# The last modulation columns on VectorE during QKV, and a tenth place for expert matrices

## The chip, the cores and the metric

The kernel runs on one core of one Trainium2 chip. The metric is the device time of one execution in microseconds, lower is better. All arithmetic is float32.

## The reference, cut to what matters

Two layers over 256 context and 256 latent tokens of width 1024 (512 rows, four tiles of 128). Layer 0 mixes tokens with a bidirectional Mamba-2 SSD, layer 1 with differential attention; each is followed by a mixture of 16 experts, two per token. Every sub-layer is modulated by six vectors per layer, made from the conditioning:

```
mod_l = silu(c)     @ ada_w[i] + ada_b[i]      # latent tokens, 6 * 1024 columns
mod_c = silu(c_ctx) @ ada_w[i] + ada_b[i]      # context tokens
sh1, sc1, g1, sh2, sc2, g2 = split(mod_l, 6)
hl  = rmsnorm(xl) * (1 + sc1) + sh1            # before the mixer
xl  = xl + g1 * mixer(hl)
hl2 = rmsnorm(xl) * (1 + sc2) + sh2            # before the experts
xl  = xl + g2 * experts(hl2)
```

In the second layer only latent rows leave the mixer, so of its columns g1, sh2, sc2 and g2 only the row of `c` is used. An expert has three matrices of 2 MB: gate, up (1024 x 512) and down (512 x 1024).

## The kernel before, in words

The program is written by hand, one instruction stream for each engine (TensorE `pe`, VectorE `v`, ScalarE `act`, GpSimd `pool`, and `sp`, the queue that issues nearly all loads). Each stream runs in its written order; semaphores join them. Nothing plans or reorders. The stages follow each other: modulation and first norm (to some 125 us), the SSD walk (to 456), output projection (to 580), first experts (to 830), QKV (844 to 990), attention (to 1085), second experts (to the end).

**The modulation columns.** The 12,288 columns are six groups q of 2048 (q = 0 to 2 are layer 0, q = 3 to 5 layer 1). Group 0 is made at the start. Groups 1 to 5 are made in the SSD walk in 40 pieces: piece p has 128 rows of `ada_w` and 2048 columns (1 MB, two loads of 512 KB by `ada_piece_sync`, L326, into two alternating buffers), and four products on TensorE add it into bank 7 of PSUM (`ada_piece_tensor`, L334; 32 output rows, of which two are used, latent and context; each float32 product shows as two records). After eight pieces VectorE adds the bias (`ada_vector`, L344) and ScalarE stores the rows to `mod_d` in memory (`ada_scalar`, L353). Later stages load from `mod_d`.

**The walk.** 16 iterations i, one for each 128 channels. On TensorE one has a projection of x (L822), the transposes (L843), the states (L866), a projection of z (L833), and the outputs (L882, L886). `ada_turn` (L675) puts a piece at three turns of an iteration: after the projection of x, after that of z, and after the outputs; every ninth turn is skipped. The same turns stand in `fused_sync` on `sp`, where the third comes after the load of the decay rows of iteration i + 2, which waits for the outputs of iteration i.

**Experts.** Class `Moe` sorts the rows into groups of 128 slots (ten in the first stage, seven in the second), and each group uses one to four experts. The 48 matrices of a stage are loaded once each, in an order of first use (`seq`), into nine places of 2 MB: six of `ring`, and parts of other buffers (`SLOTS`, `SLOTS + 1`, `NINTH` in the first stage, `SPLIT`, in three pieces, in the second). `sync_first` (L1742) loads those of experts 0 to 2, whose number doesn't depend on the routing, each behind the wait that frees its place; `sync_rest` (L1750) loads the others when the routing is known (`PERM`, `WEIGHTS`), each after the last use of the matrix that was in its place. In the first stage eight matrices are loaded ahead and `NINTH` takes the ninth after the routing; in the second the ninth goes to `SPLIT` after the routing.

**QKV** (`att_tensor`, L2577). 20 products of 128 x 512 outputs (L2591), m_ = 0 to 19: query halves for the two latent tiles, key halves and value halves for four tiles. After products 12 to 17 come the transposes of one normed query or key tile each (L2562), after 18 and 19 the first scores. VectorE (`att_vector`, L2708) norms and rotates six tiles, n = 0 to 5: two of queries (ready after products 2 and 3), four of keys (products 8 to 11; n = 2, 3 are context and aren't rotated). GpSimd gives the reciprocal roots between. `att_sync` (L2515) loads the six weight blocks, then the two of the output projection, then a gate row.

## Time and profile before

| | us |
|---|---|
| median of 3 runs | 1308.67 (1308.54 to 1314.22) |
| the profiled execution's own time | 1307.49 |
| its span | 1305.8 |
| TensorE busy | 1241.2 (95%) |
| VectorE busy | 555.7 (43%) |
| ScalarE busy | 376.3 (29%) |
| GpSimd busy | 200.7 (15%) |
| moved by DMA | 347.86 MB, mean 266 GB/s |
| mean granted clock of TensorE | 0.993 of full |

How to read it: the span is the time from the first to the last instruction; the profiled execution took 1.7 us more than its span. "Idle before, releaser" is the time an engine stood still in front of an instruction, and what ended it. In a row of windows the numbers after the stretch are its length and the busy time of TensorE's products, of its weight loads, of VectorE, ScalarE and GpSimd, each with its count; then the granted clock, the busy share of the 16 DMA engines, and GB/s.

### The profile page before, as it was taken

Reading aid. Unit: us, or ns where it says so; the run is one execution under the profiler, and the core shown is the slowest. Engines: PE = TensorE matmul, PEld = TensorE weight load, DVE = VectorE, ACT = ScalarE, POOL = GpSimd, SP = SyncE. Lnnn points to the kernel's source line nnn. Section 1 sums busy time; section 2 is a strip of 40 time slices with the busy share of each in tenths; the row PEclk is TensorE's granted clock in tenths of the full one; section 3 lists DMA queues with packets and bytes.
Section 4 is the critical chain, followed back from the end, with each engine's and each line's share of the span. In section 5 each row is a group of like instructions: output and inputs, shape, how many; then the busy total and the mean of one; then the engine's idle time right before and its main releaser. Section 6 shows DMA issues by size and latency. Waiting matters only on the chain.

```text
span 1305.8 us, 14975 instructions
## 1 busy us (share of the span) xinstructions
PE 1241.2 (95%) x5951; PEld 580.8 (44%) x5951; DVE 555.7 (43%) x907; ACT 376.3 (29%) x706; POOL 200.7 (15%) x192
## 2 busy tenths in 40 slices
PE   5899999999999999999999998899999899999977
PEld 3344444444454444574343432344444556444322
DVE  1448375756657412462111111662606755232213
ACT  2334666575756400111010100320115521000000
POOL 1001234343434310001000000311200300000000
PEclk9999999999999999999999999999999999999989
DMA  9334557766575583089999999970006237999997
GB/s 359 113 133 153 182 203 260 257 236 238 190 259 177 210 323 129 32 352 372 426 427 426 427 430 426 390 281 1 1 16 266 110 126 315 423 426 426 425 416 292
DMA packets 81454, 347.86 MB, mean 266 GB/s; under 512 B 9721, under 2 KB 27817, under 8 KB 66657
## 3 DMA queue, kind: packets, MB, share of 16 engines
q1 hardware_dynamic: 74603, 327.47, 64.1%
q10 hardware_dynamic: 4268, 10.44, 2.1%
q0 software_dynamic: 2512, 8.97, 1.7%
q8 instruction: 48, 0.79, 0.3%
q14 instruction: 23, 0.19, 0.0%
HBM read 337.67 MB, written 9.18 MB: 266 GB/s over the span
## 4 chain that ended last, share of the span: by engine, by line
PE 78%; DMA 9%; DVE 7%; SPq 2%; ACT 2%; issue 1%; ACTq 1%; POOL 0%; DVEq 0%; POOLq 0%
PE psum L1801 21%; PE psum L2591 11%; PE psum L822 10%; PE psum L833 8%; PE psum L1169 6%; DMA ring<-in_moe_w_down 5%; PE psum L340 3%; PE psum L1885 2%; PE psum L2643 2%; PE psum L866 2%; PE psum L886 2%; SPq L1773 1%; DMA arena<-mod_d 1%; PE psum L1939 1%; PE psum L882 1%
## 5 line engine op out<-in xcount | busy, mean ns | idle before, releaser
L1801 PE MATMUL psum<-ring,arena 128*32 128x512 f32 (+2 forms) x1504 | 318.6, 603 | 10.0 <-DMA ring<-in_moe_w_down 7.5
L1801 PEld LDWEIGHTS psum<-ring,arena 128*32 128x32 f32 (+2 forms) x1504 | 96.0, 125 | 175.1 <-issue 158.5
L822 PE MATMUL psum<-hT,ring 128*128 128x512 f32 x384 | 169.7, 596 | 0.0
L2591 PE MATMUL psum<-ring,hT 128*128 128x512 f32 x320 | 138.9, 592 | 0.0
L1169 PE MATMUL psum<-ring 128*128 128x512 f32 x256 | 112.1, 594 | 4.2 <-DVE X L1229 2.9
L833 PE MATMUL psum<-hT,ring 128*128 128x512 f32 x256 | 112.5, 592 | 0.0
L822 PEld LDWEIGHTS psum<-hT,ring 128*128 128x128 f32 x384 | 71.3, 190 | 91.3 <-issue 91.3
L1801 PE MATMUL psum<-arena 128*32 128x512 f32 (+2 forms) x304 | 109.3, 594 | 0.0
L1027 DVE SCALAR_TENSOR_TENSOR arena<-arena,cols 128x512 f32<-128x512 f32 x96 | 92.8, 966 | 3.4
L2591 PEld LDWEIGHTS psum<-ring,hT 128*128 128x128 f32 x320 | 60.1, 190 | 73.0 <-issue 72.2
L2011 ACT ACTIVATE arena<-psum 128x512 f32<-128x512 f32 x17 | 18.2, 1068 | 215.4 <-PE psum L1801 215.4
L965 ACT ACTIVATE ring<-ring,dts 128x128 f32<-128x128 f32 x256 | 76.5, 387 | 0.5
L1169 PEld LDWEIGHTS psum<-ring 128*128 128x128 f32 x256 | 47.8, 190 | 62.5 <-issue 56.6
L833 PEld LDWEIGHTS psum<-hT,ring 128*128 128x128 f32 x256 | 47.4, 190 | 53.6 <-issue 53.6
L2060 DVE TENSOR_TENSOR arena<-arena,psum 128x512 f32<-128x512 f32 x17 | 18.2, 1069 | 108.5 <-PE psum L1801 108.5
L1801 PE MATMUL psum<-hT,arena 128*64 128x512 f32 (+2 forms) x144 | 63.5, 594 | 0.0
L1057 DVE COPY X<-psum 128x256 f32<-128x256 f32 x16 | 6.8, 424 | 107.0 <-PE psum L866 107.0
L1801 PEld LDWEIGHTS psum<-arena 128*32 128x32 f32 (+2 forms) x304 | 31.3, 126 | 42.6 <-issue 42.3
L2671 ACT ACTIVATE arena<-psum 128x512 f32<-128x512 f32 x20 | 11.9, 597 | 116.6 <-PE psum L2591 116.6
L1115 POOL TENSOR_TENSOR arena<-arena,dts 128x512 f32<-128x512 f32 x32 | 39.1, 1243 | 38.3 <-ACT arena L947 38.3
L1106 POOL TENSOR_TENSOR ring<-ring,arena 128x512 f32<-128x512 f32 x16 | 20.3, 1271 | 148.1 <-ACT ring L958 148.1
L340 PE MATMUL psum<-arena,X 128*32 128x512 f32 x240 | 42.4, 605 | 0.0
(360 smaller groups left out, 1588.7 us busy)
## 6 DMA issues: line engine op xcount, KB each, us to landing
ring<-in_moe_w_gate SPq DMA_DIRECT2D x23, 2048.0 KB, 16.6
ring<-in_moe_w_up SPq DMA_DIRECT2D x22, 2048.0 KB, 18.0
ring<-in_moe_w_down SPq DMA_DIRECT2D x20, 2048.0 KB, 21.6
arena<-in_ada_w SPq DMA_DIRECT2D x60, 512.0 KB, 5.9
ring<-in_ssd_w_in SPq DMA_DIRECT2D x16, 1024.0 KB, 8.1
ring<-acs_d SPq DMA_DIRECT2D x16, 1024.0 KB, 7.0
ring<-in_da_w_in SPq DMA_DIRECT2D x6, 2048.0 KB, 16.5
ring<-in_ada_w SPq DMA_DIRECT2D x20, 512.0 KB, 5.1
```

The lines of the kernel that those rows point to most:

```text
L340: m = pe.matmul(psum[32 * j:32 * j + 32, 7, :], c_sil[:, k, :], ada_buf[p % 2][j // 2][:, (j % 2) * NB:(j % 2 + 1) * NB], start=(k == 0), ...
L822: mm = pe.matmul(psum[:, bank, :], w_[:, k, c0:c0 + P], hT[:, k, :], start=(k == 0), stop=(k == KD - 1))
L833: mm = pe.matmul(psum[:, 1, :], zw[b % 2][:, k, (i % 2) * P:(i % 2 + 1) * P], hT[:, k, :], start=(k == 0), stop=(k == KD - 1))
L866: mm = pe.matmul(dst, Bt[:, c_, g * STATE:(g + 1) * STATE], src, start=True, stop=True)
L886: mm = pe.matmul(dst[r, :], S[:, lv, P * d_ + 64 * hh:P * d_ + 64 * hh + 64], EC[i % 2][:, n, hh * P:(hh + 1) * P], start=False, stop=(las ...
L965: m = act.activation(x_, x_, ACT.Relu, scale=-1.0, bias=ebias[:, b:b + 1])
L1027: ins = v.scalar_tensor_tensor(out=o, in0=u_[:, :, tap:tap + SEG], scalar=cols[:, t_:t_ + 1], in1=o, op0=ALU.mult, op1=ALU.add)
L1115: pool.tensor_tensor(out=XW[:, :, n, :].rearrange("p c (h e) -> p c h e", h=2), in0=xtok[:, i % 2].rearrange("p c (h e) -> p c h e", h=2), ...
L1169: mm = pe.matmul(psum[:, wout_bank(n), :], yT[:, k, t * P:(t + 1) * P], slot((4 + k // KD, k // KD)[half], KD)[:, k % KD, :], start=(k == ...
L1801: mm = pe.matmul(psum[rows, dst, :], lhsT[:, k, rows], weight(s_, a, k, part), start=(k == 0), stop=(k == a - 1))
L1885: m = pe.matmul(psum[:, k // 4, (k % 4) * P:(k % 4 + 1) * P], self.norm.rows[t][:, k * P:(k + 1) * P], (token_mask[j] if n else self.mask0 ...
L2591: mm = pe.matmul(psum[:, 4 + m_ % 2, :], hT[:, k, t * P:(t + 1) * P], slot(qkv_slot[n], KD)[:, k, :], start=(k == 0), stop=(k == KD - 1))
```

## The change

Five things change.

- The pieces of groups 4 and 5 (16 of 40) leave the walk. The other 24 are placed at the first turn of each iteration and the second turn of every even one. The three copies come at i = 5, 10, 15.
- Groups 4 and 5 are made in QKV, for the latent row alone. `sp` loads 1 MB pieces into the two halves of a new buffer `spare`; VectorE multiplies each by the column of `silu(c)` (one number for each partition) and adds it into `late_acc` (128 x 2048, in the part of X that held context tiles). After eight pieces TensorE sums over the partitions by four products with ones, VectorE adds the bias and `sp` stores the row. TensorE waits for pieces 0 to 7 after product 9, for 8 to 15 after product 18.
- `spare` is also the tenth place for expert matrices, and the first to be filled in both stages.
- Room for it: the triangle matrices and the columns move into X, `ones` becomes a broadcast column, the strict triangle of the router comes from memory instead of a subtraction, and the descriptor space of GpSimd's DMAs becomes 2048 bytes.
- Small things that follow: a third SiLU at the start (`c_keep`), a wait of `sp` for the last transposed product before X is reloaded, a wait of GpSimd for the stored rows.

```diff
-        tri_up = sb("tri_up", [P, P])
-        tri_lo = sb("tri_lo", [P, P])
-        ones = sb("ones", [P, P])
-        cols = sb("cols", [P, 176])
+        spare = sb("spare", [P, SLOT])
+        c_keep = small[:, 24:32]
+        tri_up, tri_lo = X[:, 1, 768:768 + P], X[:, 1, 768 + P:D]
+        cols = X[:, 2, 0:176]
+        ones = small[:, 16:17].broadcast_to([P, P])
...
+            act.activation(c_keep, cols[:, CC0:CC0 + KD], ACT.Silu).then_inc(csil_ready, 1)
...
-        PIECES = 5 * KD
+        PIECES, WALKED = 3 * KD, 3
+        ADA_COPY = {5: 1, 10: 2, 15: 3}
...
         def ada_turn(do, eng, p, i, n):
-            if (3 * i + n) % (KD + 1) == KD or p >= PIECES:
+            if n == 2 or (n == 1 and i % 2) or p >= PIECES:
                 return p
...
-            sp.wait_ge(mod_out, 160)
+            sp.wait_ge(mod_out, 32 * WALKED)
...
+            sp.wait_ge(yT_ready, NT)
             sp.dma_start(X[:, 2:4, :], x[0].rearrange("(t p) n -> p t n", p=P)).then_inc(x_back, 16)
...
+                eng.dma_start(self.strict, strict_d).then_inc(self.s["router_in"], 16)
...
-                   ((0, 1), (0, 2), (1, 1), (1, 2), (0, 0), (1, 0), (2, 1), (2, 2)),
-                   (4, 5, 0, 2, 1, 3, 7, 6, NINTH), (2, 2, 1, 1, 2, 2, 0, 0, 0, 0), None, None, (nA, nS, ngb, nh, njunk))
+                   ((0, 1), (0, 2), (1, 1), (1, 2), (0, 0), (1, 0), (2, 1), (2, 2), (2, 0)),
+                   (SPARE, 4, 5, 0, 2, 1, 3, 7, 6, NINTH), (2, 2, 1, 1, 2, 2, 0, 0, 0, 0, 0), None, None, (nA, nS, ngb, nh, njunk))
...
+        def late_piece_sync(sp, p):
+            q, k = WALKED + 1 + p // KD, p % KD
+            if p >= 2:
+                sp.wait_ge(ada_used, PIECES + p - 1)
+            sp.dma_start(late_buf(p), ada_w[1, k * P:(k + 1) * P, (q % 3) * 2 * D:(q % 3 + 1) * 2 * D]).then_inc(ada_in[p % 2], 16)
...
+        def late_piece_vector(v, p):
+            q, k = WALKED + 1 + p // KD, p % KD
+            v.wait_ge(ada_in[p % 2], 32 * (PIECES // 2) + 16 * (p // 2) + 16)
+            if k == 0:
...
+                v.tensor_scalar(late_acc, late_buf(p), c_keep[:, k:k + 1], None, ALU.mult).then_inc(ada_used, 1)
+            else:
+                v.scalar_tensor_tensor(out=late_acc, in0=late_buf(p), scalar=c_keep[:, k:k + 1], in1=late_acc, op0=ALU.mult,
+                                       op1=ALU.add).then_inc(ada_used, 1)
+            v.wait_ge(ada_used, PIECES + p + 1)
+
+        def late_sum_tensor(pe, q, bank):
+            n = q - WALKED
+            pe.wait_ge(ada_used, PIECES + KD * n)
+            for j in range(4):
+                m = pe.matmul(psum[32 * j:32 * j + 32, bank, :], small[:, 16:17].broadcast_to([P, 32]), late_acc[:, j * NB:(j + 1) * NB],
+                              start=True, stop=True)
+            m.then_inc(ada_done, 1)
...
+            sp.wait_ge(*moe0.used(*moe0.holder[SPARE]))
+            for p in range(2):
+                late_piece_sync(sp, p)
             for n in range(2):
                 sp.wait_ge(A["qkv_mm"], (2, 4)[n])
                 load(sp, out_slot[n], blocks(da_w_out[0], n * NB), KD)
+            for p in range(2, LATE):
+                late_piece_sync(sp, p)
+                if p == 2:
+                    ada_bias_sync(sp, WALKED + 1)
+                if p == LATE - 1:
+                    late_store_sync(sp, WALKED + 1)
+                    ada_bias_sync(sp, WALKED + 2)
+            moe1.sync_first(sp, 0, ([(ada_used, PIECES + LATE)],))
+            late_store_sync(sp, WALKED + 2)
+            sp.wait_ge(mod_out, 32 * WALKED + 32)
...
+        LATE_SUM = {9: (WALKED + 1, 2), 18: (WALKED + 2, 7)}
+        LATE_VECTOR = ((0,), range(1, KD), (), range(KD, KD + 2), range(KD + 2, KD + 4), range(KD + 4, LATE))
...
+                if m_ in LATE_SUM:
+                    late_sum_tensor(pe, *LATE_SUM[m_])
                 if m_ >= FIRST_V:
+                    if m_ == FIRST_V:
+                        pe.wait_ge(ada_copied, WALKED + 2)
...
+        def late_vector(v, n):
+            if n == 2:
+                late_copy_vector(v, WALKED + 1, 2)
+            for p in LATE_VECTOR[n]:
+                late_piece_vector(v, p)
...
-                   qkv_slot[2:6] + [7] + out_slot + [6, SPLIT], [f + 1 + (s_ in out_slot) for s_, f in enumerate(qkv_fill[0:SLOTS])] + qkv_fill[SLOTS:SLOTS + 2] + [0], moe0, norm_b,
+                   [SPARE] + qkv_slot[2:6] + [7] + out_slot + [6, SPLIT],
+                   [0 if s_ == SPLIT else f + (s_ in qkv_slot) + (s_ in out_slot) for s_, f in enumerate(qkv_fill)], moe0, norm_b,
...
-            moe0.sync_first(sp, 0, ([(wo_mm, TT)], [], [(wo_mm, 2 * TT)], [], [(wo_mm, 2 * TT + 1)], []))
+            moe0.sync_first(sp, 0, ([], [(wo_mm, TT)], [], [(wo_mm, 2 * TT)], [], [(wo_mm, 2 * TT + 1)], []))
...
-            moe1.sync_first(sp, SLOTS + 2, ([moe1.routed("PERM")],))
...
-    nc = bacc.Bacc("TRN2", target_bir_lowering=False, num_devices=1)
+    nc = bacc.Bacc("TRN2", target_bir_lowering=False, num_devices=1, dynamic_dma_scratch_size=2048)
```

## Rows read from the trace of the kernel before

**Rows 1.** the page: busy times by engine, and GB/s in 40 slices of 32.6 us

```profile
PE 1241.2 (95%) x5951; PEld 580.8 (44%) x5951; DVE 555.7 (43%) x907; ACT 376.3 (29%) x706; POOL 200.7 (15%) x192
...
GB/s 359 113 133 153 182 203 260 257 236 238 190 259 177 210 323 129 32 352 372 426 427 426 427 430 426 390 281 1 1 16 266 110 126 315 423 426 426 425 416 292
```

**Rows 2.** waits of TensorE: 125:490 (first), 580:850 (two), 1080:1306 (last)

```profile
PE psum L340 <- DMA arena<-in_ada_w: 2.0, 1, 2.0
...
PE psum L1985 <- DVE hT L2295: 2.5, 1, 2.5
PE psum L1801 <- DMA ring<-in_moe_w_down: 1.7, 1, 1.7
...
PE psum L1801 <- DMA ring<-in_moe_w_down: 5.8, 2, 3.9
```

**Rows 3.** chain of waits, 278:322: start us, us, what

```profile
278.37 7.06 PE psum L822 x16
...
295.20 1.00 PE psum L340 x8
...
299.52 7.07 PE psum L822 x16
...
319.68 2.34 PE psum L822 x5
```

**Rows 4.** timeline, 299:322: VectorE, ScalarE

```profile
309.52 0.42 DVE L1057 COPY X<-psum 128x256 f32<-128x256 f32 x1 [7.79 <-PE psum L866]
...
301.83 0.63 ACT L939 ACTIVATE arena<-arena 128x512 f32<-128x512 f32 x1 [5.84 <-DVE arena L1074]
```

**Rows 5.** chain of waits, near the walk's end

```profile
421.54 4.87 DMA arena<-in_ada_w
```

**Rows 6.** chain of waits, at the start

```profile
13.71 0.31 ACT X L275 x2
```

**Rows 7.** chain of waits over the whole span, QKV stage

```profile
859.82 75.54 PE psum L2591 x176
```

**Rows 8.** timeline of VectorE, QKV stage

```profile
890.73 1.22 DVE L2740 TENSOR_TENSOR arena<-arena 128x1024 f32<-128x1024 f32 x1
```

**Rows 9.** by source line: ns min/median/max of each form

```profile
L1027 DVE SCALAR_TENSOR_TENSOR arena<-arena,cols x96: 750/752/1808, 56.5 to 420.5; 128x512 f32<-128x512 f32 x96
...
L2295 DVE SCALAR_TENSOR_TENSOR hT<-hT,arena x2: 1283/1283/1283, 827.7 to 831.4; 128x1024 f32<-128x1024 f32 x2
...
L2294 DVE TENSOR_SCALAR hT<-hT,arena x2: 753/754/754, 826.9 to 830.6; 128x1024 f32<-128x1024 f32 x2
```

**Rows 10.** transfers: of line L332, and the DMA issues in 843:1000

```profile
DMA to landing us min/median/max: 3.6/5.7/11.8
...
ring<-in_da_w_out SPq DMA_DIRECT2D x2, 2048.0 KB, 8.0
```

**Rows 11.** timeline of TensorE, 1245:1252

```profile
1250.70 1.93 PE L1801 MATMUL psum<-ring,arena 128*32 128x512 f32 x8 [3.85 <-DMA ring<-in_moe_w_down]
```

**Rows 12.** windows: stretch, us, busy by engine, PEclk, DMA share, GB/s

```profile
1250.00:1256.00 6.00, 5.30 (x36) 1.41 (x40) 0.00 (x0) 0.00 (x0) 0.00 (x0) 0.64 0.99 421
795.00:800.00 5.00, 3.29 (x8) 0.77 (x8) 0.00 (x0) 0.00 (x0) 0.00 (x0) 0.69 1.03 436
```

**Rows 13.** windows of the expert stages, same columns

```profile
495.00:555.00 60.00, 60.00 (x173) 28.97 (x172) 20.74 (x47) 7.40 (x13) 2.23 (x6) 1.00 0.22 88
...
600.00:790.00 190.00, 190.00 (x1012) 70.47 (x1012) 29.54 (x42) 17.84 (x25) 6.54 (x7) 1.00 1.01 427
...
1100.00:1290.00 190.00, 179.71 (x1192) 70.91 (x1192) 49.80 (x98) 9.31 (x11) 0.00 (x0) 0.98 1.01 421
```

**Rows 14.** chain of waits, at the end

```profile
1277.93 14.20 DMA ring<-in_moe_w_down
```

**Rows 15.** gathers: timeline of GpSimd, 795:845, and the chain

```profile
817.17 0.95 POOL L2263 DMA_INDIRECT hT<-moe_y_d,arena  x1 [88.22 <-DMA moe_y_d<-arena]
...
818.42 7.90 DMA hT<-moe_y_d,arena
```

More of the change, by code:

```diff
@@ L136, in slot @@
         def slot(s, a):
-            flat = ring[:, s, :] if s < SLOTS else {SLOTS: arena[:, 4096:8192], SLOTS + 1: hT[:, :, :].rearrange("p k t -> p (k t)"), NINTH: arena[:, 0:4096]}[s]
+            flat = ring[:, s, :] if s < SLOTS else {SLOTS: arena[:, 4096:8192], SLOTS + 1: hT[:, :, :].rearrange("p k t -> p (k t)"), NINTH: arena[:, 0:4096], SPARE: spare[:, :]}[s]
             return flat.rearrange("p (a b) -> p a b", a=a)
@@ L144, in backbone @@
         up_d = nc.inline_tensor(np.triu(np.ones((P, P), np.float32)), "up_d").ap()
+        strict_d = nc.inline_tensor(np.triu(np.ones((P, P), np.float32), 1), "strict_d").ap()
         lo_d = nc.inline_tensor(np.tril(np.ones((P, P), np.float32)), "lo_d").ap()
@@ L148, in backbone @@
         full = [sem(f"slot{s}_full") for s in range(SLOTS + 3)]
-        SPLIT, NINTH = SLOTS + 2, SLOTS + 3
-        full.append(full[SPLIT])
+        SPLIT, NINTH, SPARE = SLOTS + 2, SLOTS + 3, SLOTS + 4
+        full += [full[SPLIT], sem("spare_full")]
         def split_pieces():
@@ L252, in setup_pool @@
         def setup_pool(pool):
-            pool.memset(ones[:, :], 1.0).then_inc(pool_set, 1)
             pool.memset(small[:, :], 0.0).then_inc(pool_set, 1)
             pool.memset(Xflat[:, 0:256], 0.0).then_inc(pool_set, 1)
-            pool.wait_ge(pool_set, 3)
+            pool.wait_ge(pool_set, 2)
+            pool.memset(small[:, 16:17], 1.0).then_inc(pool_set, 1)
             pool.memset(mhalf, -0.5).then_inc(pool_set, 1)
@@ L300, in keep_busy @@
             for _ in range(n):
-                pe.matmul(psum[:, bank, 0:P], ident[:, :], ones[:, :], start=True, stop=True)
+                pe.matmul(psum[:, bank, 0:P], ident[:, :], ident[:, :], start=True, stop=True)
         def ada_first_tensor(pe):
@@ L345, in ada_vector @@
             v.wait_ge(ada_used, KD * q)
-            v.wait_ge(adab_in, 16 + 64 * (3 if q <= 3 else 5))
+            v.wait_ge(adab_in, 16 + 64 * WALKED)
             if q == 1:
@@ L697, in fused_sync @@
                 ada_piece_sync(sp, p)
-            for q in range(1, 4):
+            for q in range(1, WALKED + 1):
                 ada_bias_sync(sp, q)
@@ L1007, in fused_scalar @@
                     conv_copy(act, BCN + i + 2)
-                if i and i % 3 == 0:
-                    ada_scalar(act, i // 3)
                 if i + 1 < NT:
@@ L1013, in fused_scalar @@
                     z_scalar(act, i + 1)
+                if i in ADA_COPY:
+                    ada_scalar(act, ADA_COPY[i])
             yT_scalar(act, NT - 1)
@@ L1091, in fused_vector @@
                     gated_vector(v, step, i - 1)
-                if i and i % 3 == 0:
-                    ada_vector(v, i // 3)
+                if i in ADA_COPY:
+                    ada_vector(v, ADA_COPY[i])
                 states_vector(v, step, i)
@@ L1183, in wout_tensor @@
             for t_ in range(TT):
-                mm = pe.matmul(psum[:, 3, t_:t_ + 1], acc[:, t_ * P:(t_ + 1) * P], ones[:, 0:1], start=True, stop=True)
+                mm = pe.matmul(psum[:, 3, t_:t_ + 1], acc[:, t_ * P:(t_ + 1) * P], small[:, 16:17], start=True, stop=True)
             mm.then_inc(y_scale, 1)
@@ L1481, in shift_tensor @@
                 pe.wait_ge(cols_ready, self.cols_at + 1)
-                pe.matmul(psum[:, self.bank, 256:256 + NE * len(self.conds)], ones[:, :], self.rwR.rearrange("p c e -> p (c e)"), start=True, stop=True)
+                pe.matmul(psum[:, self.bank, 256:256 + NE * len(self.conds)], ones, self.rwR.rearrange("p c e -> p (c e)"), start=True, stop=True)
             def router_pool_start(self, pool, step):
@@ L1751, in sync_rest @@
                 expert = {r: r for r in range(NPRE)}
-                for m, r in self.seq[len(self.slots) - (not self.masked):]:
+                for m, r in self.seq[len(self.slots) - 1:]:
                     if len(expert) == NPRE:
@@ L1761, in sync_rest @@
                         sp.wait_ge(*self.used(*self.after[(m, r)]))
-                    else:
+                    elif not self.masked:
                         sp.wait_ge(*self.routed("WEIGHTS"))
@@ L2529, in att_pool @@
             pool.wait_ge(A["small_in"], 144)
-            pool.memset(mhalf16, -0.5).then_inc(A["const"], 1)
-            pool.wait_ge(A["const"], 1)
+            step(pool.memset(mhalf16, -0.5))
             for n in range(6):
@@ L2726, in att_vector @@
                     ins.then_inc(done, 1)
+                    late_vector(v, n)
                     continue
```

55 lines of the change are left out of this document (36 added, 19 removed).

## The prediction

> **What bounds the kernel now.** I read the page's busy shares first: TensorE is busy for 95% of the span [rows 1]. So time can go only where TensorE does less or waits less. The chain of waits, then asked for by stretch, shows one line after another of TensorE with hardly an idle piece. The waits of TensorE give the rest: 2.0 us in the SSD walk, a few in the first mixture of experts, and in the second several for transfers, of which the largest group is 5.8 us [rows 2] and all four together are 11.6 us. So the walk is bound by what TensorE issues, each expert stage is bound by TensorE at first and by its weights at the end, and the QKV stage by TensorE alone.
>
> **The change part by part.** The frame is the profiled execution: span 1305.8 us, its own time 1307.5 us; the median of the runs is 1.2 us above that.
>
> **1. The walk.** One piece (four column products, eight records) takes 1.00 us of the chain [rows 3]. An iteration with three pieces lasts 299.52 - 278.37 = 21.15 us, one with two 319.68 - 299.52 = 20.16 us [rows 3]: the difference is the piece itself, nothing hides it. 40 pieces become 24, so 16 x 1.00 = 16.0 us go. New iterations hold two pieces or one (20.16 and 19.16 us). Does something else become late there? VectorE waits 7.8 us for the states of this iteration and ScalarE 5.8 us for the gated product [rows 4]; both wait for TensorE's course, so a loss of 1.0 to 2.0 us an iteration stays inside that slack. The second to last piece waits 2.0 us for its transfer, because a DMA of the third turn is issued only after the outputs of its iteration; the chain shows it as a DMA piece of 4.87 us [rows 5]. The new walk has no third turn: every piece is asked for at least a third of an iteration before its use. That is another -2.0. The three copies move to iterations 5, 10 and 15; two of them now wait for a piece of their own iteration, but what follows on VectorE is the state copy, which waits for a later product anyway: 0. SP's queue loses 32 half-pieces and two bias loads: 0, it waits for TensorE.
>
> **2. Start.** A third SiLU of 8 columns stands before the squares on ScalarE. Two take 0.31 us and the squares follow at once on the chain [rows 6]: +0.2. The missing memset, broadcast ones, and the triangle matrix from memory: 0 (bounds -0.5 and +0.5).
>
> **3. The late pieces in QKV.** TensorE gets two sums, each four products of the form of a piece: +2.0. The pieces are work of VectorE now, and TensorE waits for them at one point: after product 9 of 20 it needs pieces 0 to 7. In the trace of before, products 2 to 12 run back to back from 859.82 in 75.54 us, 6.87 us each [rows 7]; product 9 ends at 859.82 + 8 x 6.87 = 914.8. VectorE ends its second query tile at 890.73 + 1.22 = 891.95 [rows 8]. A piece with its addition is a form that costs 0.75 us for 512 columns and 1.28 us for 1024 [rows 9], so 0.53 for each further 512, and 2.34 us for 2048. Piece 0 needs no addition; that form does 1024 columns in 0.75 us [rows 9], so 1.3 us for 2048. It stands before the second query tile, so the run of pieces 1 to 7 starts at 891.95 + 1.3 = 893.3. Piece 1 is there and is used at 895.7. Piece 3 could be asked for only now, since there are two buffers, and each later pair again waits for its own buffer: transfer plus use per pair. A transfer of 1 MB: a half of 512 KB lands in 3.6 us at least and 5.7 in the median, a 2 MB one on an idle queue in 8.0 [rows 10]; 512 KB cost 1.2 us at the rate of 427 GB/s [rows 13], so 3.6 + 1.2 = 4.8 from one side and 8.0 - 2.5 = 5.5 from the other. I take 5.2. Three pairs then take 3 x (5.2 + 2.34 + 0.1 issue) = 22.9, and piece 7 is used at 918.6: TensorE waits 918.6 - 914.8 = +3.9 us, a pace of 3.8 us a piece. Bounds: 0, with 3.6 us a transfer; 12, with 8.0 and with the 3 us that 2048 columns would cost if contention made them a quarter slower. I stay near the rows of this size.
>
> By the Trainium skill ("DMA: Bandwidth & Descriptors", Anatomy of one DMA) a transfer costs some 2.0 us plus its bytes over 436 GB/s, so 4.4 us here as an estimate; the stall would be 1.5 us. Its Bandwidth section has 6.15 us for 1 MB, which would make 6.7 us. No row here shows a lone transfer of 1 MB in this stage; the sum goes by the rows.
>
> A stall also costs clock. Late in the second expert stage TensorE was idle for 3.85 us up to 1250.70 [rows 11], and from 1250 to 1256 its granted clock was 0.64, a mean of its two levels [rows 12]: 6 x 0.36 = 2.2 us lost. For a 3.9 us stall I take +2.1 (0 to 2.2).
>
> What waits behind the pieces on VectorE: the key tiles. A tile takes 7.1 us without the rotation and 12.3 us with it, in the timeline of [rows 8]. Pushed to 918.7, the four of them and pieces 8 to 15 end about 980; their transposes on TensorE are due from 956, 964, 971 and 979 (one product each 7.7 us, stall and sum included) and their tiles are ready at 926, 935, 951, 968; the second sum after product 18 is due at 987. All are in time, with 7 us or more. On SP the pieces stand ahead of the second stage's weights, which waited for the last product at 990 before, and end before that: 0. Their 16.8 MB go into a stretch that moved 1 GB/s in two slices (the 28th and 29th) [rows 1]. The gate row, the new wait of GpSimd for the stored row, the two stores of 8 KB: behind products, 0. The sum here is 2.0 + 3.9 + 2.1 = +8.0.
>
> **4. First experts, the tenth place.** DMA moves 427 GB/s without a gap from 600 to 790, so a matrix of 2.10 MB costs 4.9 us; from 495 to 555 it moved 88 GB/s [rows 13]. The new place is filled there, at once after the last small load, so all weights from the thirteenth on land 4.9 us earlier against TensorE. TensorE waited 1.7 us for a down matrix at the end of the stage [rows 2] and ran at 0.69 from 795 to 800 [rows 12], another 1.6 us: both go, -3.3. The rows of group 8 are then stored with less in front of them and the gathers behind it hold TensorE for 2.5 us [rows 2]; half of that, -1.2. Sum -4.5, bounds -1.7 and -5.8.
>
> **5. Second experts.** 39 matrices instead of 40 come after the routing. The DMA moved 421 GB/s from 1100 to 1290, and TensorE was idle for 10.3 us of that [rows 13]. The chain's last transfer lands at 1292.1 and 13.7 us of fixed work follow to the span's end [rows 14]. The first load moves into the nearly empty QKV stretch, so one matrix fewer in a full one: -4.9. It can't be more, since 11.6 us of waits are left to eat and only 4.9 are removed; bounds 0 (if places, not bytes, hold the loads) and -4.9.
>
> **Sum.** -16.0 - 2.0 + 0.2 + 8.0 - 4.5 - 4.9 = -19.2. 1307.5 - 19.2 = 1288.3; against the median of the runs, 1289.5 us.
>
> **The rivals.** The median frame is used in all.
> No stall: transfers of 3.6 us, or tiles finished earlier. The 6.0 us go: 1283.5. For it: the stretch is empty of other traffic. Against: even 4.8 us a transfer leave a stall.
> The place brings nothing: loads are held by places being free, as SP's queue waits for TensorE in both stages. -9.4 is missing: 1298.9. Against it the full DMA stretches.
> The walk stops at 20.16 us an iteration, the shortest seen, by a chain through VectorE and the decay rows: 8 iterations give back 1.0 us: 1297.5. The slack speaks against it.
> Slower than before: the pace of the pieces. If the two buffers did not overlap, a piece would cost transfer and use in turn, 5.7 + 2.3 = 8.0 us. Place: TensorE's wait after product 9, then the one after product 18. The first stall is 6 times the pace less 19.1, the second 4 times the pace less 20.2, where positive; at 8.0 that is 28.9 + 11.8 = 40.7 us. Without any stall the change gives 25.2 us, less 2.1 for the clock: 1326.3. It decides from 6.2 us a piece. For it: the chain of waits on VectorE after each piece; against it: two buffers with a semaphore each.
> Also slower: the smaller descriptor space of GpSimd's queue. It issues 8 gathers, 1.25 us apart, and one lands in 7.9 us [rows 15]; were each held until the one before has landed, 7 x (7.9 - 1.25) = 47 us would come, some 1335. The trace shows no such wait and doesn't tell the space that they need.
>
> **How the numbers follow.** Forecast 0.55, no stall 0.16, place without gain 0.14, walk held 0.06, pace 0.05, gathers 0.04. The forecast's own bounds (stall 0 to 6, experts ±4) give 1284 to 1296; with no stall below and the missing gain above, 1281 to 1300 holds eight in ten. Faster by over 0.5% (under 1302.1; half a per cent is about what a measurement tells from no change) are the first four, 0.91, and a little of the pace case: 0.92; the range around no change is reached only by paces of 5.7 to 6.8: 0.03; slower 0.05.
>
> **What would show it.** Iterations of 20.2 and 19.2 us; no transfer on the chain near the end of the walk; a wait of TensorE of 2 to 6 us before the first late sum, with a fall of the clock behind it; late pieces 3.8 us apart in runs, each 2.3 us on VectorE; first experts with no wait on a down matrix; waits of some 6 to 7 us left in the second. Wrong would be a walk iteration with a new wait, pieces over 6 us apart, a second wait after product 18, or gathers held on GpSimd.

## The result, and the profile after

The changed kernel takes 1301.19 us (median of 11 runs, 1298.13 to 1304.74); beside it the kernel before took 1309.68 us (median of 11). The ratio is 0.9924, 95% interval [0.9908, 0.9940]: 8.5 us gained by the medians, 7.9 to 12.0 by the interval, about half of the 19.2 forecast. The time is 1.2 us above the upper end of the range (1281 to 1300). The profiled execution took 1301.31 us, its span is 1299.6.

The page of the changed kernel, busy times and GB/s in 40 slices of 32.5 us, to be read beside [rows 1]:

```profile
PE 1227.6 (94%) x5839; PEld 580.6 (45%) x5839; DVE 604.2 (46%) x921; ACT 376.6 (29%) x707; POOL 203.5 (16%) x192
...
GB/s 357 117 134 154 156 145 186 195 199 223 165 138 216 152 306 146 57 348 425 425 428 427 427 428 416 392 261 211 81 185 292 108 104 300 425 427 425 425 417 288
```

TensorE is busy for 13.6 us less, yet the span is only 6.2 us shorter: 7.4 us of waits came in place of work. VectorE is busy for 48.5 us more, and the transfers of the late pieces now stand in the 28th to 30th slice (211, 81 and 185 GB/s, where there were 1, 1 and 16).

The waits of TensorE, in total, times and longest, in the stretches of [rows 2]:

```profile
PE psum L843 <- ACT arena L939: 7.0, 2, 5.6
...
PE psum L2545 <- DVE X L2536: 2.9, 1, 2.9
...
PE psum L1986 <- DVE hT L2296: 3.8, 1, 3.8
PE psum L1854 <- DMA arena<-moe_h_d,arena: 2.1, 1, 2.1
...
PE psum L1802 <- DMA ring<-in_moe_w_gate: 4.1, 1, 4.1
PE psum L1802 <- DMA ring<-in_moe_w_down: 3.8, 1, 3.8
PE psum L1844 <- DMA spare<-in_moe_w_down: 1.8, 1, 1.8
```

The longest of the first one is new: before, TensorE waited there once, for 1.5 us at the walk's start. Now it also stands still for 5.6 us near the end of the walk, until ScalarE has done the SiLU of the convolution. The timeline of TensorE there:

```profile
389.54 7.13 PE L822 MATMUL psum<-hT,ring 128*128 128x512 f32 x16
...
408.70 1.06 PE L342 MATMUL psum<-arena,X 128*32 128x512 f32 x8
415.35 1.11 PE L843 MATMUL psum<-ident,arena 128*128 128x128 f32 x4 [5.58 <-ACT arena L939]
416.25 2.77 PE L866 MATMUL psum<-arena 128*128 128x256 f32 x8
```

Up to 389.54 the walk runs as forecast: its iterations start 20.16 and 19.16 us apart. From 389.54 on L822 stands no more, since the last two iterations have no projection (7.1 us each): TensorE comes that much earlier to the transposes of L843. The granted clock falls during the wait and stays low behind it, a mean of its two levels, 1.2 and 2.4 GHz, in each of these windows (columns as in [rows 12]):

```profile
409.00:416.00 7.00, 1.42 (x11) 0.66 (x4) 5.50 (x5) 1.32 (x3) 1.27 (x2) 0.73 0.85 281
416.00:422.00 6.00, 6.00 (x19) 3.96 (x18) 2.84 (x4) 5.96 (x14) 4.16 (x3) 0.75 0.98 370
```

So L866 takes 2.77 instead of 1.47 us. The timeline of VectorE and ScalarE shows why the SiLU is late. One round, from one copy (L931) to the next:

```profile
384.41 0.58 ACT L931 ACTIVATE arena<-psum 128x512 f32<-128x512 f32 x1
...
385.02 0.55 DVE L1024 TENSOR_SCALAR arena<-arena,X 128x512 f32<-128x512 f32 x1 [0.75 <-ACT arena L931]
385.61 4.57 DVE L1027 SCALAR_TENSOR_TENSOR arena<-arena,X 128x512 f32<-128x512 f32 x4
390.09 2.28 DVE L1049 TENSOR_TENSOR ring<-ring,arena 128x2048 f32<-128x2048 f32 x1
392.41 1.23 DVE L1051 TENSOR_TENSOR ring<-ring 128x1024 f32<-128x1024 f32 x1
393.55 0.74 DVE L1072 SCALAR_TENSOR_TENSOR arena<-arena,psum 128x512 f32<-128x512 f32 x1
394.33 0.69 DVE L1074 TENSOR_TENSOR arena<-arena 128x512 f32<-128x512 f32 x1
...
395.11 0.63 ACT L939 ACTIVATE arena<-arena 128x512 f32<-128x512 f32 x1 [5.83 <-DVE arena L1074]
...
399.28 4.78 ACT L965 ACTIVATE ring<-ring,dts 128x128 f32<-128x128 f32 x16
403.96 0.58 ACT L931 ACTIVATE arena<-psum 128x512 f32<-128x512 f32 x1
```

It closes. The copy lets VectorE begin the convolution. Then come the masks of the decay rows (L1049, L1051) and the gated product (L1072, L1074). ScalarE waits for that with its next SiLU (L939); behind it come the table load, the exponentials and 16 Relus (L965), and behind them the next copy. 403.96 - 384.41 = 19.55 us, and in nine of the last twelve iterations the SiLUs stand exactly 19.55 or 19.56 us apart; TensorE takes 19.66 for an iteration on average. Before, the SiLUs stood 19.5 to 22.4 us apart, led by TensorE.

Stages from the timelines of 13 profiles (all but e2_few and e3_few_order), each from the first product of one part to that of the next (us; walk: L822 of the second iteration to L1170; first experts: to the first QKV product; second experts: from their first expert product to the span's end):

| kernel | start | walk | to experts | first experts | QKV to router | second experts |
|---|---|---|---|---|---|---|
| before | 132.3 | 308.7 | 150.7 | 252.5 | 220.8 | 216.7 |
| changed | 133.6 | 298.0 | 150.6 | 249.4 | 230.8 | 212.9 |
| e1_order | 131.0 | 292.0 | 151.3 | 251.5 | 230.7 | 212.2 |
| e4_sum10 | 130.7 | 299.1 | 150.9 | 252.1 | 223.0 | 213.1 |
| e5_nine | 130.7 | 298.9 | 151.5 | 251.6 | 228.9 | 216.5 |
| e6_before_order | 131.0 | 308.2 | 151.1 | 252.1 | 224.0 | 216.5 |
| e7_order_sum10 | 130.2 | 292.0 | 152.7 | 249.4 | 224.7 | 212.5 |
| e8_halves | 131.4 | 298.2 | 150.3 | 249.9 | 225.0 | 213.3 |
| e9_order_halves | 131.7 | 292.0 | 155.0 | 250.4 | 224.5 | 212.7 |
| e10_all | 132.4 | 292.0 | 152.4 | 252.1 | 223.0 | 212.7 |
| e11_changed_again | 134.4 | 298.1 | 150.9 | 251.8 | 229.1 | 213.0 |
| e12_nine_first | 133.4 | 297.9 | 150.7 | 253.4 | 230.8 | 212.8 |
| e13_before_space | 129.5 | 308.5 | 150.2 | 251.9 | 221.7 | 216.6 |

From router to experts it is 24.1 us in all (25.8 in the last). Each row is one profiled execution.

### The profile page after: what moved, and what is told of

Same layout as the page of the kernel before. It is cut to its first block, busy times and chain, and to the rows that moved or that the text cites. A ratio compares the mean times of both kernels' runs of the same rounds, so it can differ in the third digit from the quotient of the medians.

```text
span 1299.6 us, 14781 instructions
## 1 busy us (share of the span) xinstructions
PE 1227.6 (94%) x5839; PEld 580.6 (45%) x5839; DVE 604.2 (46%) x921; ACT 376.6 (29%) x707; POOL 203.5 (16%) x192
## 4 chain that ended last, share of the span: by engine, by line
PE 72%; DVE 11%; DMA 6%; ACT 4%; SPq 3%; issue 2%; ACTq 1%; POOL 1%; DVEq 0%; POOLq 0%
PE psum L1802 23%; PE psum L822 9%; PE psum L2658 7%; PE psum L833 7%; PE psum L1170 6%; SPq L1774 3%; PE psum L1886 2%; PE psum L2715 2%; DVE arena L1027 2%; PE psum L1940 2%; PE psum L342 1%; PE psum L866 1%; ACT ring L965 1%; PE psum L886 1%; DMA arena<-mod_d 1%
## 5 line engine op out<-in xcount | busy, mean ns | idle before, releaser
L1802 PE MATMUL psum<-ring,arena 128*32 128x512 f32 (+2 forms) x1328 | 306.1, 598 | 9.5 <-DMA ring<-in_moe_w_gate 4.1
L822 PE MATMUL psum<-hT,ring 128*128 128x512 f32 x384 | 169.7, 596 | 0.0
L1802 PEld LDWEIGHTS psum<-ring,arena 128*32 128x32 f32 (+2 forms) x1328 | 92.8, 125 | 171.3 <-issue 158.9
L2658 PE MATMUL psum<-ring,hT 128*128 128x512 f32 x320 | 141.8, 602 | 0.0
L1170 PE MATMUL psum<-ring 128*128 128x512 f32 x256 | 112.1, 594 | 4.1 <-DVE X L1230 2.9
L822 PEld LDWEIGHTS psum<-hT,ring 128*128 128x128 f32 x384 | 71.3, 190 | 85.3 <-issue 85.3
L1027 DVE SCALAR_TENSOR_TENSOR arena<-arena,X 128x512 f32<-128x512 f32 x96 | 92.8, 967 | 3.4
L1802 PE MATMUL psum<-spare,arena 128*64 128x512 f32 (+1 forms) x192 | 85.0, 594 | 0.0
L1802 PE MATMUL psum<-arena 128*32 128x512 f32 (+1 forms) x264 | 84.8, 593 | 0.0
L965 ACT ACTIVATE ring<-ring,dts 128x128 f32<-128x128 f32 x256 | 76.5, 387 | 0.5
L1170 PEld LDWEIGHTS psum<-ring 128*128 128x128 f32 x256 | 47.8, 190 | 62.5 <-issue 56.4
L1802 PE MATMUL psum<-hT,arena 128*32 128x512 f32 (+2 forms) x160 | 58.3, 605 | 0.0
L1061 DVE TENSOR_TENSOR X<-X,arena 128x256 f32<-128x256 f32 x32 | 45.0, 1407 | 1.1
L1115 POOL TENSOR_TENSOR arena<-arena,dts 128x512 f32<-128x512 f32 x32 | 39.2, 1245 | 35.8 <-ACT arena L947 35.8
L1057 DVE COPY X<-psum 128x256 f32<-128x256 f32 x16 | 6.8, 425 | 73.4 <-PE psum L866 73.4
## 6 DMA issues: line engine op xcount, KB each, us to landing
arena<-in_moe_w_gate SPq DMA_DIRECT2D x6, 2048.0 KB, 16.5
```

Of the source, the lines that this page charges most:

```text
L822: mm = pe.matmul(psum[:, bank, :], w_[:, k, c0:c0 + P], hT[:, k, :], start=(k == 0), stop=(k == KD - 1))
L965: m = act.activation(x_, x_, ACT.Relu, scale=-1.0, bias=ebias[:, b:b + 1])
L1027: ins = v.scalar_tensor_tensor(out=o, in0=u_[:, :, tap:tap + SEG], scalar=cols[:, t_:t_ + 1], in1=o, op0=ALU.mult, op1=ALU.add)
L1061: step(v.tensor_tensor(out=m4, in0=i4, in1=d4, op=ALU.mult))
L1115: pool.tensor_tensor(out=XW[:, :, n, :].rearrange("p c (h e) -> p c h e", h=2), in0=xtok[:, i % 2].rearrange("p c (h e) -> p c h e", h=2), ...
L1170: mm = pe.matmul(psum[:, wout_bank(n), :], yT[:, k, t * P:(t + 1) * P], slot((4 + k // KD, k // KD)[half], KD)[:, k % KD, :], start=(k == ...
```

## The experiments

**e1_order: the gated product ahead of the masks.**

```diff
 for i in range(NT):
-    if i:
-        gated_vector(v, step, i - 1)
     if i in ADA_COPY:
         ada_vector(v, ADA_COPY[i])
     states_vector(v, step, i)
     if i + 2 < NT:
         conv_vector(v, step, BCN + i + 2)
+    gated_vector(v, step, i)
     if i + 1 < NT:
         decay_vector(v, step, i + 1)
-gated_vector(v, step, NT - 1)
```

> The changed kernel with one edit: in the walk VectorE does the gated product of head pair i before it masks the decay rows of pair i+1, not after. Theory (loop): near the end of the walk TensorE waits 5.6 us for the SiLU of the convolution, because ScalarE and VectorE go round in a loop of 19.55 us per iteration (copy 0.58, five convolution steps 5.1, mask 2.3 + 1.2, gated product 0.7 + 0.7 on VectorE, then SiLU, scale, table, two exponentials, 16 Relus on ScalarE). The edit takes the 3.5 us of the masks out of the loop, 16 us an iteration; the wait of 5.6 us and the 1.9 us of slow products behind it go: 1301.2 - 7.5 = 1293.7 (1292 to 1296), no wait of TensorE on that SiLU over 1 us after iteration 0. Rival (copies): the three copies of modulation rows in iterations 5, 10 and 15 hold VectorE; they stand where they stood, so the wait stays: 1301. Rival (transfers): the decay rows come late from memory; also 1301.

1294.44 us, ratio to the kernel before 0.9880 [0.9851, 0.9908] (all ratios below are to it). The walk takes 292.0 us, 6.0 less. The wait is 1.3 us, and the clock holds:

```profile
408.44 0.66 PE L843 MATMUL psum<-ident,arena 128*128 128x128 f32 x4 [1.30 <-ACT arena L939]
408.93 1.47 PE L866 MATMUL psum<-arena 128*128 128x256 f32 x8
```

The copies and the transfers stood where they had stood, so both rivals fall.

**e2_few and e3_few_order: the loop laid bare.** In both nearly all products of the walked pieces are left out (their sums are wrong then):

```diff
-for j in range(4):
-    m = pe.matmul(psum[32 * j:32 * j + 32, 7, :], ...
+for j in range(4 if k == 0 else 1):
+    w_ = NB if k == 0 else 16
+    m = pe.matmul(psum[32 * j:32 * j + 32, 7, 0:w_], ...
```

> The changed kernel without nearly all the products of the 24 walked pieces: of each piece that isn't the first of its group only one product of 16 columns is left (the modulations of these groups are wrong then, and with them the routing behind the walk, so only the walk is compared). Transfers, waits and copies stay. From the first product of pair 2's projection to the first of the output projection the changed kernel takes 298.0 us (133.6 to 431.6). Theory (loop): the walk is held by the loop of 19.55 us through ScalarE and VectorE, not by what TensorE issues; 21 pieces fewer win next to nothing: 292 to 297 us, and TensorE waits for the SiLU in nearly every iteration, some 1.4 us each. Rival (TensorE sets the pace, the wait at the end is a mishap of its own): 298.0 - 21 x 1.0 = 277 us, or less by the 7.5 us.

> As the kernel with few products, and VectorE's gated product of pair i before the masks of pair i+1. Theory (loop): the loop takes 16 us now and TensorE's own course of 18.2 us an iteration sets the pace again: 298.0 - 7.5 - 20 = 270 us (267 to 274) for the stretch. Rival (the order on VectorE plays no part): the same stretch as the kernel with few products alone.

Their whole time says nothing here, for the routing is another. The walk took 295.2 us in e2_few (298.0 in the changed kernel) and 276.0 us with the order changed as well. So 21 us of TensorE's work, taken out of a walk of 298, won 2.8 us; its waits for the SiLU grew from 7.0 us (two) to 17.2 (eleven). All waits of TensorE in this walk for the SiLU, and two of ScalarE's:

```profile
PE psum L844 <- ACT arena L940: 17.2, 11, 8.2
...
312.55 0.63 ACT L940 ACTIVATE arena<-arena 128x512 f32<-128x512 f32 x1 [5.84 <-DVE arena L1075]
332.10 0.63 ACT L940 ACTIVATE arena<-arena 128x512 f32<-128x512 f32 x1 [5.84 <-DVE arena L1075]
```

332.10 - 312.55 = 19.55 us: the loop's own pace, whatever TensorE does. With the new order as well the walk takes 276.0 us, 19.2 less, though 2 us over the end of the range that I had expected: waits of 4.2 us for the SiLU stay.

**e4_sum10: the first late sum one product later.**

```diff
-LATE_SUM = {9: (WALKED + 1, 2), 18: (WALKED + 2, 7)}
+LATE_SUM = {10: (WALKED + 1, 2), 18: (WALKED + 2, 7)}
```

> The changed kernel with one edit: the first late sum on TensorE stands after product 10 of QKV instead of after product 9. Theory (stall): TensorE is 2.9 us too early for piece 7, and the clock falls behind that wait (the sum takes 1.78 instead of 1.00 us, the next products 1.1 us longer). One product of 6.9 us more covers the wait: 1301.2 - 4.8 = 1296.4 (1295.5 to 1298). Rival (key tiles): VectorE's copy of the sum moves some 4 us later and the key tiles behind it with it, so the wait turns up at the transposes from product 12 on and nothing is won: 1301 to 1303.

1294.26 us, ratio 0.9884 [0.9857, 0.9912], 2.1 us better than the theory and below its range. The sum, in the changed kernel and then here, by the timeline of TensorE:

```profile
906.91 1.78 PE L2545 MATMUL psum<-X,small 128*32 128x512 f32 x8 [2.94 <-DVE X L2536]
```

```profile
910.21 1.07 PE L2545 MATMUL psum<-X,small 128*32 128x512 f32 x8
```

The stage is 7.8 us shorter than in the changed kernel's profile. That is more than the stall: the granted clock was low at three places of the stage in the changed kernel and at none here. Windows of the changed kernel, at the stage's start, at the stall, and in attention:

```profile
831.00:836.00 5.00, 5.00 (x15) 2.46 (x14) 4.90 (x9) 2.66 (x6) 0.18 (x1) 0.66 1.05 387
...
905.00:910.00 5.00, 3.09 (x10) 1.00 (x11) 4.31 (x3) 0.00 (x0) 0.45 (x2) 0.71 0.76 275
...
1028.00:1033.00 5.00, 3.95 (x23) 3.96 (x24) 2.72 (x5) 2.35 (x6) 2.21 (x4) 0.70 0.01 3
```

and the same places here:

```profile
832.00:837.00 5.00, 5.00 (x18) 2.74 (x19) 4.90 (x9) 2.65 (x6) 0.04 (x1) 1.00 1.05 387
905.00:910.00 5.00, 5.00 (x13) 2.06 (x11) 3.70 (x3) 0.00 (x0) 1.06 (x2) 1.00 0.66 226
...
1026.00:1031.00 5.00, 3.99 (x28) 3.06 (x27) 2.07 (x3) 1.79 (x3) 3.02 (x5) 1.00 0.45 94
```

Between the start of product 9 and that of product 12 the changed kernel lost 4.8 us to this one, by the stall and the slow products behind it. The other 3.0 were lost at the first and the third place. That isn't the edit's doing: e7_order_sum10 has the edit and a clock of 0.66 at the stage's start, and e11_changed_again, without it, has 1.00 there. No wait for a key tile took the stall's place: the room that the prediction counted for the tiles (7 us or more) was enough.

**e6_before_order: the same order in the kernel before.** The edit is that of e1_order.

> The kernel before with one edit: VectorE's gated product of head pair i before the masks of pair i+1. Theory (the loop binds only once the pieces are gone): before, TensorE's own 20.7 us an iteration stand over the loop's 19.55, and its only wait in the walk's end is one for a piece, 2.0 us: no change, -0.5 to +0.5 us. Rival (the order is a gain of its own, whatever the pieces): -5 us or more, 1304.5 or less where the kernel before takes 1309.5.

1309.72 us, ratio 0.9991 [0.9974, 1.0007]; walk 308.2 against 308.7. While TensorE had 20.8 us of work an iteration the order of the two steps was worth nothing; with the change it is.

**e7_order_sum10: both edits.**

> The changed kernel with both edits: gated product before the masks in the walk, first late sum after product 10. Theory (two separate losses, of two stages): the gains add, -6.8 and -4.8 from 1301.2: 1289.6 (1286.5 to 1291). Rival (one of them is given back later, by waits for weights in the expert stages, since TensorE comes to them earlier and the transfers don't): 1292 to 1294, with the waits of TensorE for weights in the second experts 3 us or more longer than the changed kernel's 9.7.

1289.57 us, ratio 0.9844 [0.9817, 0.9871]: the gains add, and the waits for weights in the second experts are 9.6 us as in the changed kernel. This beats both kernels. That it lies where the prediction had put the change itself (1289.5) is chance: that forecast still had a stall of 6.0 us in it, which is gone here.

**e8_halves: the late pieces cut in two.**

```diff
-return spare[:, (p % 2) * 2 * D:(p % 2 + 1) * 2 * D]
+return spare[:, (p % 4) * D:(p % 4 + 1) * D]
...
+    v.wait_ge(ada_used, PIECES + p - 1)
+    v.scalar_tensor_tensor(out=acc_, in0=late_buf(p), scalar=c_keep[:, k:k + 1], in1=acc_, ...)
```

> The changed kernel with the late pieces cut in two: four buffers of 1024 columns in the same place, each with a transfer of 512 KB, each used by an instruction of 1024 columns. In the changed kernel a piece costs transfer plus use over two buffers, (5.0 + 2.4) / 2 = 3.7 us. Theory (the pace is that sum): with halves (3.7 + 1.3 + 0.1) / 4 = 1.28 us a half at best, where the use itself takes 1.28 and the bytes 1.23 us: 2.6 to 3.0 us a piece; piece 7 is used some 5 to 7 us earlier, the stall of 2.9 us and the clock's share behind it go: 1301.2 - 4.5 = 1296.7 (1295.5 to 1298). Rival (the transfers of one queue go one after another, each with its fixed cost): 3.7 us a half or more, so 7.4 us a piece, and stalls of 20 us and more: 1325.

1297.18 us, ratio 0.9900 [0.9873, 0.9926]. Pieces 1 to 7 take 21.7 us, 3.1 each, a little over the 2.6 to 3.0 expected, for a half landed after 5.1 us in the median and not after 3.7. Four halves on VectorE, in the timeline:

```profile
892.54 1.29 DVE L2542 SCALAR_TENSOR_TENSOR X<-spare,small,X 128x1024 f32<-128x1024 f32 x1 [0.68 <-DMA spare<-in_ada_w]
894.32 3.81 DVE L2542 SCALAR_TENSOR_TENSOR X<-spare,small,X 128x1024 f32<-128x1024 f32 x3 [0.49 <-DMA spare<-in_ada_w]
```

The wait before the sum is 0.2 us. Halves that land 5.1 us after their issue are used 1.55 us apart, so the transfers of this queue overlapped; that rival falls.

**e9_order_halves and e10_all: is there one stall or several shares?**

> The changed kernel with the gated product before the masks in the walk and with the late pieces cut in two; the first late sum stays after product 9. Theory (the QKV stall can be taken away from either end, by a later use or by faster pieces, with one result): the gains add, -6.8 and -4.0 from 1301.2: 1290.4 (1288 to 1292.5), that is the same as the kernel with the order and the later sum, 1289.6. Rival (VectorE's 3 us of earlier release move the key tiles forward, and something behind them with it): under 1288.

> All three edits together: gated product before the masks, halves of pieces, first late sum after product 10. Theory (there is one stall in QKV, and it is gone with either edit): no more than the kernels with two edits, 1289.6 (1288 to 1291.5). Rival (each edit takes its own share of it): 1285.5, another 4 us less.

e9_order_halves: 1291.58 us, ratio 0.9859 [0.9833, 0.9885]; e10_all: 1289.78 us, ratio 0.9848 [0.9823, 0.9872]. Both are where the theories had put them. Three edits bring no more than two: there was one stall, and it can be taken away from either end.

**e5_nine and e12_nine_first: the tenth place.** e5_nine gives the spare rows back to the late pieces alone, in both stages; e12_nine_first does so for the first experts only. The list of places of the latter (the waits of `sp` that go with it are left out here):

```diff
-(..., (2, 1), (2, 2), (2, 0)), (SPARE, 4, 5, 0, 2, 1, 3, 7, 6, NINTH)
+(..., (2, 1), (2, 2)), (4, 5, 0, 2, 1, 3, 7, 6, NINTH)
```

> The changed kernel with nine expert matrix places, as before: the spare rows hold only late pieces, the experts' order of loads is that of before. Theory (place as forecast, bytes): the first experts lose the 4.8 us that they gained, the second 3.8, and the 1.7 us that the first gather lost in the changed kernel come back: 1301.2 + 6.9 = 1308 (1305 to 1310); the last transfer of the second stage lands some 4 us later against the end of attention. Rival (places, not bytes, hold the loads, and the stages moved by other things): 1300 to 1303. A second reading of the same run: if the first gather's landing stays at 8.0 us, the extra place had nothing to do with its being slower.

> The changed kernel with nine places in the first experts and ten in the second. With nine in both, the median was 6.3 us above the changed kernel's, and the second stage 3.6 us longer in the profiles. Theory (each stage has its own price for a matrix that can't be loaded ahead): 2.7 us from the first, 1303.9 (1302.5 to 1305.5). Rival 1 (as forecast, 4.9 us of bytes less what waits allow: 4.5): 1305.7 or more. Rival 2 (only the second stage gains): 1301.2.

e5_nine: 1307.54 us, ratio 0.9982 [0.9962, 1.0002]; e12_nine_first: 1303.11 us, ratio 0.9944 [0.9925, 0.9964]. So without the tenth place only 2.3 us of the gain are left (the kernel before took 1309.87 beside it), and the rival, at 1300 to 1303, falls. The second experts take 216.5 to 216.7 us in the four kernels with nine places and 212.2 to 213.3 in the nine with ten: 3.8 us, with hardly any spread. The first experts take 252.3 us on average in the five with nine (251.6 to 253.4) and 250.8 in the eight with ten (249.4 to 252.1). By the medians the place is worth 1.9 us in the first and 4.4 in the second. The 1.9 is barely clear of nothing: the interval of e12_nine_first overlaps that of the changed kernel, and the ranges of the first experts overlap as well.

**e13_before_space: the descriptor space.**

```diff
-nc = bacc.Bacc("TRN2", target_bir_lowering=False, num_devices=1)
+nc = bacc.Bacc("TRN2", target_bir_lowering=False, num_devices=1, dynamic_dma_scratch_size=2048)
```

> The kernel before with one edit: the descriptor space of GpSimd's queue is 2048 instead of its default, as in the changed kernel. In the profiles of the kernel before and of the one with its order edited, GpSimd starts its third gather of the first experts 5.3 us after the second; in every kernel that carries the change, with nine places or with ten, 6.3 to 7.1 us, and TensorE waits 1.4 to 2.2 us for the first gather instead of 0.4 or less. Theory (the smaller space holds a gather's descriptors back): here too 7 us and a wait of about 2.1 us; 1309.7 + 1.7 = 1311.4 (1310 to 1314). Rival (the first gather is slower for another reason, such as the addresses or the loads beside it): 5.3 us, a wait of at most 0.4, and 1309.7 (1308.5 to 1310.9).

1311.65 us, which is in the theory's range, but the kernel before took 1311.45 beside it: ratio 1.0006 [0.9990, 1.0022]. TensorE waits 1.2 us for the gather, between theory and rival. e8_halves and e9_order_halves, with the small space, waited 0.3 and 0.2 us, and e5_nine, with nine places, 2.1. So my theory falls: TensorE has the first gathered rows 7.3 to 9.3 us after its first expert product, and neither the place nor the space decides which. What does stays open; it is worth 2 us at most.

**e11_changed_again: the changed kernel once more.**

> The changed kernel itself once more, beside the others on one chip. The first products of the walk stood at 132.3 us in the kernel before and at 133.6 us in the changed one, and at 130.2 to 131.4 in the kernels with one edit, which have the third SiLU as well. Theory (the start's 1.3 us is the spread of runs, not the SiLU): 130.2 to 132.3 here; the wait for the SiLU of the convolution at the end of the walk is 5 to 6 us again; median 1300 to 1302.5. Rival (the start is of the change): 133.6 again.

1300.44 us, ratio 0.9927 [0.9901, 0.9953]; walk 298.1 us, as in the first profile of this kernel, with a wait of 5.4 us. The start came at 134.4, outside what I had expected and above the first profile. So it isn't set by the code alone: three kernels without the third SiLU stand at 129.5 to 132.3 (mean 130.9), ten with it at 130.2 to 134.4 (mean 132.0).

## Why the prediction was wrong

By its own steps, forecast and found (differences of means of the table's columns, between kernels that differ in that step):

| step | forecast | found |
|---|---|---|
| 1. walk | -18.0 | -10.1 (308.5 to 298.4) |
| 2. start | +0.2 | +1.0, within the spread |
| 3. QKV | +8.0 | +7.9 (222.2 to 230.1) |
| 4. first experts | -4.5 | -1.5 |
| 5. second experts | -4.9 | -3.8 |
| sum | -19.2 | -6.5 in the profiles, -8.5 by the medians |

The two sums differ since each profile is one execution: those of the three kernels with the walk of before were 1.1 to 5.8 us faster than their medians (1307.49, 1308.66 and 1305.88 us), those of the changed kernel 0.1 and 2.6 us slower.

**Step 1 failed, and with it the forecast.** Its sentence was "both wait for TensorE's course, so a loss of 1.0 to 2.0 us an iteration stays inside that slack"; and "The slack speaks against it" stood beside the right rival, the walk held by a chain through VectorE and the decay rows, to which I gave 0.06. The 16.0 us of the pieces were right: where the loop doesn't hold TensorE (292.0 us) the walk is 16.5 us shorter than before. I took the 5.84 us that ScalarE waits for the gated product [rows 4] as slack against TensorE. It is none: ScalarE waits there for VectorE inside the loop, and the same wait stands in e2_few, where TensorE has 21 us less to do. A wait inside a loop doesn't shrink when the loop becomes the bound. VectorE's wait for the states was true slack, and it is what shrank: [rows 4] shows 7.79 us in one iteration, and all 16 together were 107.0 us before and 73.4 in the changed kernel. From the two pages:

```profile
L1057 DVE COPY X<-psum 128x256 f32<-128x256 f32 x16 | 6.8, 424 | 107.0 <-PE psum L866 107.0
```

```profile
L1057 DVE COPY X<-psum 128x256 f32<-128x256 f32 x16 | 6.8, 425 | 73.4 <-PE psum L866 73.4
```

What was missing was the loop's length, and it could be had before: add up ScalarE's and VectorE's instructions of one iteration along their dependences, 19.55 us, against new iterations of 19.66 us on TensorE. Even at the rival's place I had the wrong price: the loop doesn't cost 1.0 us in every second iteration, it costs in the last ones, where TensorE's own work falls by 7.1 us and the loop's doesn't. The new order gives 6.4 us of the missing 7.9 back (292.0 in all four kernels that have it).

The -2.0 for the last transfer was mostly not there to be had, for a second wait stood behind the first. In the trace of before, the SiLU that TensorE needed next ended at 426.24 + 0.63 = 426.87 and TensorE came at 427.45, held by the transfer: without that wait it would have waited 1.4 us there for the SiLU, and only 0.6 was to be had. The four kernels with the new order keep such a wait of 1.3 us. The row, from the timeline of ScalarE before the change:

```profile
426.24 0.63 ACT L939 ACTIVATE arena<-arena 128x512 f32<-128x512 f32 x1 [5.48 <-DVE arena L1074]
```

**Step 3 was right** in kind and nearly in size. By the means of the table the two sums cost 1.9 us (222.2 without late pieces, 224.0 in the five kernels whose stall is gone or nearly gone) and the stall with its clock 6.0. That these are the 2.0 and 6.0 of the forecast is in part luck, for the means hold falls of the clock elsewhere in the stage (see e4_sum10). Three kernels have a granted clock of 1.00 through the whole stage: before with 220.8, e4_sum10 and e10_all with 223.0; the two sums cost 2.2. From the start of product 9 to that of product 12 the five kernels with the stall take 4.5 to 6.3 us more than e4_sum10, 5.3 on average: 2.9 for the wait and 2.4 for the slow products behind it, where I had 3.9 and 2.1. The wait was shorter since the three pairs of pieces took 22.1 us and not 22.9. (The upper bound that I gave for the stall was wrong: with 8.0 us a transfer it is 12 us without the slower use, 15 with it.) The transfers and the use, by DMA issues and by source line (ns, min/median/max):

```profile
spare<-in_ada_w SPq DMA_DIRECT2D x16, 1024.0 KB, 5.0
```

```profile
L2536 DVE SCALAR_TENSOR_TENSOR X<-spare,small,X x14: 2344/2352/2352, 882.4 to 967.0; 128x2048 f32<-128x2048 f32 x14
```

5.0 us against 5.2 taken from the rows, and 2.35 against 2.34. The Trainium skill ("DMA: Bandwidth & Descriptors", Anatomy of one DMA) gives 4.4 us as an estimate, and its Bandwidth section 6.15, both for transfers that GpSimd issues; the trace, with transfers from `sp` and two in flight, lies between. Halves of 512 KB in e8_halves, up to four in flight, took 5.1.

**Step 4 was mis-sized.** The wait for the down matrix (1.7) went, as forecast. The 1.6 us of clock didn't come back: in the changed kernel it is 1.00 from 795 to 800, but 0.66 from 804 to 809, and over the stage the mean granted clock is 0.991 in the five kernels with nine places and 0.988 in the eight with ten. And TensorE's wait for the added rows at the stage's end (L1986), of which I let half go, grew: 3.8 instead of 2.5 us [rows 2], 2.7 to 5.5 in the eight kernels with ten places and 1.2 to 2.7 in the five with nine. It ends by stores, gathers and VectorE. My reading is that these hardly move when TensorE comes earlier, so the wait grows by what TensorE gains, the same mistake as in step 1; no edit was made that tests it.

**Step 5 was right in kind**, -3.8 of the -4.9 for one matrix of 2.10 MB. The waits for weights are 9.7 us after 11.6, where 6 to 7 were to be left; why not all of the 4.9 came isn't shown.

**The signs and the rivals.** The iterations, the stall and its clock, and the pace of the pieces were as described; of the signs of being wrong one came, the new wait in a walk iteration. The stall was there, so that rival falls; the place brings 6.3 us by the medians of e5_nine and the changed kernel, so that one falls too. Nothing made the kernel slower: the pieces came every 3.7 us, far from the 6.2, and e13_before_space shows no cost of the descriptor space.

## What to carry to other kernels

Before work is taken from the engine that sets the pace, write down the next loop: follow the in-order queues of the other engines through one iteration until they close, and add up the instructions. If the pacing engine's new iteration comes near that sum or under it, the gain stops there; a wait between two engines of this loop is no slack. Look apart at the iterations that differ, the last ones above all, and in loops like this try the order of two independent steps on one engine: it was worth 6.8 us here by the medians (6.0 in the walk's profile), where the change brought 8.5.

## What was not expected of the hardware

VectorE's multiplication of 256 columns from two places in SBUF (L1061) took 0.42 us at least, 0.75 in the median before and 1.44 in the changed kernel, where 30 of its 32 records overlap a product of GpSimd, against 18 before. In the timelines of VectorE and GpSimd one that began at 401.37 ended at 403.38, 0.29 us after GpSimd's had ended:

```profile
401.37 2.01 DVE L1061 TENSOR_TENSOR X<-X,arena 128x256 f32<-128x256 f32 x1
...
400.55 2.54 POOL L1108 TENSOR_TENSOR ring<-ring,arena 128x1024 f32<-128x1024 f32 x1
```

The Trainium skill ("SBUF — State Buffer", SBUF: two separate sides) has it that the two engines share a pair of ports which one instruction holds to its end; these rows agree. It cost nothing in this iteration, for VectorE waited 0.75 us for ScalarE's copy behind it.

A wait costs more than its length, in both places. In QKV a stall of 2.7 to 3.2 us cost 4.5 to 6.3 us, in the five kernels that have it; in the walk a wait longer by 4.3 us (5.6 against 1.3) cost 6.4. The rest is slow products behind the wait: the granted clock was 0.71 from 905 to 910 and 0.75 from 416 to 422, means of its two levels of 1.2 and 2.4 GHz.

The clock also fell where no wait was new, and not in every execution of like code: at the start of QKV it was 0.66 in the changed kernel and 1.00 in e11_changed_again, the same kernel. Such a fall cost 1.5 to 1.7 us, and it moves the difference of two single profiles by as much; what decides whether it comes is open. Over whole runs the slower ones show the lower clock: of the kernel before, beside e1_order, 0.987 with 1314.81 us and 0.995 with 1304.77.
